# Output projection of a decoder trunk in three rounded products, with w_out loaded early by column halves

## The chip, the cores and the metric

One core of a Trainium2 chip runs the whole kernel. The metric is the time of one execution on the device in microseconds (us), as the median of several runs. The engines are TensorE (PE), VectorE (DVE), ScalarE (ACT), GpSimd (POOL, used only to build constants) and SyncE (SP), whose in-order queue issues all transfers. Every engine works through its own queue in order and waits on semaphores.

## The reference

Two layers over 256 tokens of width 1024, float32. Each layer is a mixer and a mixture of experts, both as residual branches:

```python
def reference(x, ...):
    for layer in range(DEPTH):
        h = rms_norm(x, norm_mix_g[layer])
        if layer % 2 == 0:      # differential + stick-breaking attention
            mix = even_mixer(h, ab_w_in[i], ..., ab_w_out[i], layer)
        else:                   # forgetting attention
            mix = odd_mixer(h, c_w_in[i], c_b_f[i], ..., c_w_out[i])
        x = x + mix
        h = rms_norm(x, norm_ffn_g[layer])
        x = x + hier_moe(h, ...)   # top-1 of 4 groups, top-2 of its 4 experts
    return x

def even_mixer(...):
    proj = h @ w_in                      # 1024 -> 3072
    ...                                  # heads, norms of q and k
    o = jnp.concatenate([from_heads(o_a), from_heads(o_b)], axis=-1)
    return o @ w_out                     # 1024 -> 1024, the output projection
```

## The kernel before

**Stages of a layer.** (1) The tokens are transposed (tokens_across) and multiplied by w_in in six units of 512 columns, two steps j each, so 12 steps. (2) Eight attention jobs j, in turns i: scores, exponentials, transposition of the probabilities or, for the stick-breaking heads B (layer 0, jobs 4 to 7), sums along the map (across), and products with the values (weighted_values). (3) The output projection (out_products) for four pieces q of the output, 128 tokens by 512 columns. (4) Residual adds, norm, router, ranks. (5) The experts: 16 in order, for 64 token slots each, in blocks of four (a quad). The weights of an expert are six units of 2 MB.

**Rounded products.** PE multiplies full float32 in two recorded instructions per product. For the input projection (all units but the first of layer 0) the kernel instead makes of each operand a rounded part (high, type float32r, a copy on ScalarE: weights_high, L656) and the remainder (low, a subtraction on VectorE: weights_low, L1050; tokens_low, L1042), and adds three products: high x high, low x high, high x low (L1556 for the units of v, L1563 for the others). The splits of unit u+1 are queued at an even step j. The output projection of before is in full float32 (L1578): oT holds the attention outputs (over the tile hn), copied out of PSUM by output (L732, ScalarE) or, for B heads, by VectorE (L1286), each with a signal o_ready.

**Slots.** Twelve slots of 2 MB each hold w_in, then expert units. Slots 0 to 5 hold w_in, 6 is free, 7 and 8 lie over qkT and v_sb with attention, 9 and 10 hold the rounded parts w_high and later w_out, 11 lies over hn and hT. Expert unit n of a lap goes to slot n. unit_loaded and unit_used are the semaphores of a slot.

**Order of the queues.** SP issues x, gains, w_in of layer 0, then small parameters (load, L462), then per layer: expert unit u after step 2u+2 into slot u, w_out (L472), slot 6, slot 7 after the last scores, slot 8 after the last attention output, slots 9 and 10 after the output projection, slot 11 after the router. From then on each unit is loaded as soon as its slot is used up. At the end of layer 0 come the units of w_in of layer 1. VectorE at a step j of the projection: root chain or weights_low, root products (L1230), the copy of the step's PSUM bank (L1253, L1244, L1250, signal proj_out), and after the copy of step 4 in layer 0 weights_low of unit 3 and make_tables, which waits for the small parameters. ScalarE at a step: weights_high, then the square of the step's q or k (L777, signal squared); in layer 0 at step 4 it waits for a sum that make_tables forms (L788). PE at step j waits for proj_out of step j-2, and adds up squares in sums (L1495), for the last of them inside step 8 in layer 1 and step 4 in layer 0. mixed_and_normed adds the four pieces to x (L921), ScalarE squares them, and tokens_across brings the sums across for the router.

## Time and profile before

| | us |
|---|---|
| median of 3 runs (1176.65 to 1177.93) | 1177.33 |
| span of the profiled execution | 1175.5 |
| layer 0 before its first expert's first product | 163.2 |
| experts of layer 0, to the last scatter | 587.7 |
| layer 1, first expert's first product | 744.3 |
| last scatter of layer 1 | 1169.2 |

The profiled execution's span runs from its first to its last instruction; the median lies 1.8 us above it, which is what lies around the span and the difference between executions together. Rows of the trace give the start and the duration in us, the engine and the line of the kernel. In a merged row "x8" stands for eight instructions, and the bracket gives the idle time before it and who ended it. PE matmul rows overlap, so the distance between starts is what a product costs in a stream.

### The profile page before, as it was taken

The page shows a single profiled execution, that of the slowest core. Times are in us where ns is not written, and L with a number is a line of the kernel's source. Part 1 is how long each engine was busy: PE and PEld are TensorE (multiplying, and loading weights), DVE is VectorE, ACT ScalarE, POOL GpSimd, SP SyncE. Part 2 cuts the span into 40 slices and gives each one's busy share as a digit, 9 for nine tenths or more (in the row PEclk, how much of TensorE's full clock was granted, in tenths as well). Part 3 has the DMA queues.
Part 4 walks back from the last instruction along what each step waited for, and adds up shares of the span by engine and source line. Part 5 has one row for each costly group of instructions (what it writes and reads, how often), then busy time and mean ns, then how long its engine had stood idle before and what let it go on. Part 6 is the DMA issues. An engine that isn't in the chain of part 4 may idle for free.

```text
span 1175.5 us, 13904 instructions
## 1 busy us (share of the span) xinstructions
PE 1131.3 (96%) x5664; PEld 517.1 (44%) x5664; DVE 431.1 (37%) x776; ACT 175.2 (15%) x347; POOL 7.2 (1%) x36
## 2 busy tenths in 40 slices
PE   8998989999999999999899999899999999999997
PEld 6985433333333333333389754333333333333332
DVE  4656253322222423222285662522223323222222
ACT  4327110000000000000063251000001000000000
POOL 2000000000000000000000000000000000000000
PEclk9999999999999999999999999999999999999999
DMA  9678289999999999999994383999999999999996
GB/s 358 160 324 335 95 324 429 428 427 428 428 430 428 429 428 428 428 428 428 414 397 154 143 345 108 396 428 428 428 428 429 428 429 429 429 428 428 428 429 261
DMA packets 53904, 439.30 MB, mean 374 GB/s; under 512 B 14192, under 2 KB 14192, under 8 KB 29296
## 3 DMA queue, kind: packets, MB, share of 16 engines
q1 hardware_dynamic: 53872, 438.85, 90.0%
q8 instruction: 22, 0.36, 0.1%
q14 instruction: 10, 0.08, 0.0%
HBM read 437.79 MB, written 1.05 MB: 373 GB/s over the span
## 4 chain that ended last, share of the span: by engine, by line
PE 85%; DMA 9%; DVE 3%; ACT 1%; SPq 1%; issue 1%; another core or an unknown queue 0%; ACTq 0%; DVEq 0%
PE bank L1682 50%; PE bank L1563 8%; PE bank L1578 5%; PE bank L1694 5%; PE bank L1661 4%; DMA ring<-in_moe_w_gate 4%; DMA ring<-in_moe_w_up 4%; PE bank L1556 4%; PE bank L1670 1%; PE bank L1725 1%; PE bank L1436 1%; PE bank L1495 1%; PE bank L1718 1%; PE bank L1387 1%; DMA ring<-in_ab_w_in 1%; PE bank L1412 1%
## 5 line engine op out<-in xcount | busy, mean ns | idle before, releaser
L1682 PE MATMUL bank<-ring,work 128*64 128x512 f32 x2304 | 510.9, 594 | 11.3 <-DVE work L1311 6.3
L1682 PEld LDWEIGHTS bank<-ring,work 128*64 128x64 f32 x2304 | 161.6, 137 | 343.6 <-issue 327.3
L1301 DVE TENSOR_SCALAR work<-work 128x512 f32<-128x512 f32 x32 | 13.7, 427 | 456.1 <-ACT work L829 456.1
L1303 DVE RECIPROCAL work<-work 128x512 f32<-128x512 f32 x32 | 107.3, 3353 | 1.1
L832 ACT ACTIVATE attention<-bank 128x512 f32<-128x512 f32 x32 | 19.1, 597 | 531.6 <-PE bank L1682 531.6
L1661 PE MATMUL bank<-x_sb,root_y 128*64 128x512 f32 x272 | 64.2, 593 | 0.0
L1308 DVE TENSOR_TENSOR work<-bank,work 128x512 f32<-128x512 f32 x32 | 22.1, 692 | 113.4 <-PE bank L1682 113.4
L1682 PE MATMUL bank<-ring_over_qk,work 128*64 128x512 f32 x256 | 57.7, 593 | 2.5 <-DMA ring_over_qk<-in_moe_w_gate 2.5
L1682 PE MATMUL bank<-ring_over_v,work 128*64 128x512 f32 x256 | 57.6, 592 | 0.0
L1682 PE MATMUL bank<-ring_spare,work 128*64 128x512 f32 x256 | 57.6, 592 | 0.0
L1578 PE MATMUL bank<-ring,hn 128*128 128x512 f32 x128 | 56.7, 595 | 0.0
L829 ACT ACTIVATE work<-bank 128x512 f32<-128x512 f32 x32 | 19.1, 597 | 227.5 <-PE bank L1682 227.5
L1050 DVE TENSOR_TENSOR w_low<-ring,w_high 128x2048 fp32r<-128x2048 f32 x22 | 49.4, 2285 | 6.7 <-ACT w_high L656 6.6
L656 ACT ACTIVATE w_high<-ring 128x2048 fp32r<-128x2048 f32 x22 | 41.0, 1901 | 11.7 <-PE bank L1563 6.2
L1694 PE MATMUL bank<-attention,root_ln 64*128 64x512 f32 x128 | 31.8, 613 | 6.3 <-ACT attention L832 6.3
L1661 PEld LDWEIGHTS bank<-x_sb,root_y 128*64 128x64 f32 x272 | 19.4, 137 | 39.2 <-issue 37.7
L1578 PEld LDWEIGHTS bank<-ring,hn 128*128 128x128 f32 x128 | 23.7, 190 | 27.5 <-issue 26.9
L1682 PEld LDWEIGHTS bank<-ring_over_qk,work 128*64 128x64 f32 x256 | 18.2, 137 | 39.7 <-issue 35.4
L1682 PEld LDWEIGHTS bank<-ring_spare,work 128*64 128x64 f32 x256 | 18.4, 137 | 36.6 <-issue 36.6
L1682 PEld LDWEIGHTS bank<-ring_over_v,work 128*64 128x64 f32 x256 | 18.4, 137 | 36.6 <-issue 35.7
L1694 PE MATMUL bank<-attention,root_x 64*128 64x512 f32 x128 | 31.8, 615 | 0.0
L1563 PE MATMUL bank<-h_high,w_high 128*128 128x256 f32 x224 | 31.2, 292 | 0.0
(242 smaller groups left out, 930.9 us busy)
## 6 DMA issues: line engine op xcount, KB each, us to landing
ring<-in_moe_w_gate SPq DMA_DIRECT2D x48, 2048.0 KB, 27.1
ring<-in_moe_w_up SPq DMA_DIRECT2D x48, 2048.0 KB, 29.2
ring<-in_moe_w_down SPq DMA_DIRECT2D x48, 2048.0 KB, 27.7
ring_over_qk<-in_moe_w_gate SPq DMA_DIRECT2D x16, 2048.0 KB, 30.4
ring_over_v<-in_moe_w_up SPq DMA_DIRECT2D x16, 2048.0 KB, 30.2
ring_spare<-in_moe_w_down SPq DMA_DIRECT2D x16, 2048.0 KB, 30.9
ring<-in_ab_w_in SPq DMA_DIRECT2D x12, 1024.0 KB, 14.9
ring<-in_c_w_in SPq DMA_DIRECT2D x12, 1024.0 KB, 14.4
```

Source lines behind the costliest of these rows:

```text
L656: act.activation(w_high[u % 2][:, part, :], win_view(u)[:, part, :], ACT.Copy).then_inc(s.w_high, 1)
L829: act.activation(sig, GATE[:, :], ACT.Exp, scale=-1.0).then_inc(s.gate_exp, 1)
L832: act.activation(y, Y[:, :], ACT.Copy).then_inc(s.y_out, 1)
L1050: tt(w_low[u][:, part, :], win_view(u)[:, part, :], w_high[u % 2][:, part, :].bitcast(F32), ALU.subtract).then_inc(s.w_low, 1)
L1303: nc.vector.reciprocal(sig, sig).then_inc(s.gate_step, 1)
L1308: tt(hid, UP[:, :], sig, ALU.mult).then_inc(s.hid_ready, 1)
L1556: last = mm(bank[j % 2][:, :], x_part[:, c, P * t:P * (t + 1)], w[:, c, :], start=(n == 0 and c == 0), stop=(final and c == NC - 1))
L1563: last = mm(bank[j % 2][:, T * half:T * (half + 1)], w[:, c, col:col + P], x_part[:, c, :], start=(n == 0 and half == 0 and c == 0), stop= ...
L1578: last = mm(out_bank(layer, q)[:, :], oT[:, c, P * t:P * (t + 1)], wout_view(c // SUB)[:, c % SUB, HALF * h:HALF * (h + 1)], start=(n == 0 ...
L1661: last = mm(MISC[SLOTS * h:SLOTS * (h + 1), :], take[:, t, :], x_sb[:, t, HALF * h:HALF * (h + 1)], start=(t == 0), stop=(t == NT - 1))
L1682: last = mm(b[SLOTS * half:SLOTS * (half + 1), :], left(h, k), expert_rhs(slot, k, half), start=(h == 0 and k == 0), stop=(h == 1 and k == ...
L1694: mm(ACC[2 * t + half][:, :], giveT[k % 2][r, P * t:P * (t + 1)], y[r, :], start=False, stop=False, skip_group_check=True).then_inc(s.scat ...
```

## The change

The output projection multiplies rounded and remainder parts. For that w_out is loaded by column halves: the first right after the input weights, the second once input unit 0 is done. ScalarE and VectorE split the halves at steps 5 and 7 of the input projection (WOUT_STEPS). The attention outputs are split as they leave PSUM: ScalarE copies them to o_high, VectorE forms o_low; the softmax outputs of layer 0 stay in full in o_rows until their norm is applied and are split after it. ScalarE's output now stands ahead of second in its turn. The pieces q are counted with the token block first (t, h = q % 2, q // 2), their products are interleaved in another order, and three of the four transposes for the router stand between or before the products of the last two pieces. The slots have another numbering in each layer: LAP lists them in the order in which they come free, and expert units are loaded in that order, the first five after steps 8, 10, 10, 12 and 12. Several semaphores are merged (logits_psum, rt_shift, rt_exp, tables_made count for two).

```diff
-OWN, OVER_QK, OVER_V, WOUT = range(UNITS, UNITS + 4)
+OVER_QK, OVER_V = 7, 8
+WIN_SLOTS = ((0, 1, 2, 3, 4, 5), (3, 4, 9, 5, 10, 6))
+HIGH_SLOTS = ((9, 10), (1, 0))
+WOUT_SLOTS = ((6, 0), (2, 3))
+WOUT_HIGH_SLOTS = ((1, 2), (4, 9))
+def lap_of(win, high, wout, wout_high):
+    return (win[3], win[4], high[0], win[5], high[1], OVER_QK, OVER_V, wout[0], wout_high[0],
+            wout[1], wout_high[1], SPARE)
+WOUT_STEPS = (5, 7)
...
 # SP
             for u in range(1, UNITS):
                 load_win(0, u)
+            load_wout(0, 0)
+            sp.wait_ge(layers[0].proj_psum, 2)
+            load_wout(0, 1)
...
-                for u in range(UNITS):
-                    sp.wait_ge(s.proj_psum, STEPS * layer + 2 * u + 2)
-                    load_unit(layer, u, u, 0)
-                load_wout(layer)
-                load_unit(layer, OWN, OWN - UNITS, 1)
+                if layer > 0:
+                    sp.wait_ge(s.proj_psum, STEPS * layer + 2)
+                    load_wout(layer, 1)
+                for i, steps_done in enumerate((8, 10, 10, STEPS, STEPS)):
+                    sp.wait_ge(s.proj_psum, STEPS * layer + steps_done)
+                    load_first(i)
                 sp.wait_ge(s.scores_psum, 2 * JOBS * (layer + 1))
-                load_unit(layer, OVER_QK, OVER_QK - UNITS, 1)
+                load_first(5)
                 sp.wait_ge(s.o_ready, JOBS * layer + JOBS)
-                load_unit(layer, OVER_V, OVER_V - UNITS, 1)
+                load_first(6)
+                sp.wait_ge(s.out_psum, 4 * layer + 2)
+                load_first(7)
+                load_first(8)
                 sp.wait_ge(s.out_psum, 4 * layer + 4)
-                for slot in (WOUT, WOUT + 1):
-                    load_unit(layer, slot, slot - UNITS, 1)
+                load_first(9)
+                load_first(10)
...
 # ScalarE
+            def out_weights_high(layer, h):
+                act.wait_ge(wout_loaded[h], 16 * (layer + 1))
+                act.wait_ge(s.proj_psum, STEPS * layer + 4 + 2 * h)
+                for i in range(2):
+                    act.activation(wout_high(layer, h)[:, part, :], wout_view(layer, h)[:, part, :],
+                                   ACT.Copy).then_inc(s.wout_high, 1)
...
+                act.activation(o_high[:, j, :], O_BANK[:, 0:T], ACT.Copy).then_inc(s.out_high, 1)
...
+                    if j in WOUT_STEPS:
+                        out_weights_high(layer, WOUT_STEPS.index(j))
...
                     if i < JOBS:
                         exponentials(layer, i)
+                    if 2 <= i < JOBS:
+                        output(layer, i - 2)
                     if 1 <= i < JOBS + 1:
                         second(layer, i - 1)
+                    if layer == 0 and i == JOBS:
+                        softmax_outputs_high(s)
+                    if i >= JOBS:
                         output(layer, i - 2)
...
 # VectorE
+            def out_weights_low(layer, h):
+                for i in range(2):
+                    dve.wait_ge(s.wout_high, 4 * layer + 2 * h + i + 1)
+                    tt(wout_low(layer, h)[:, part, :], wout_view(layer, h)[:, part, :],
+                       wout_high(layer, h)[:, part, :].bitcast(F32), ALU.subtract
+                       ).then_inc(s.wout_low, 1)
+            def output_low(layer, j):
+                tt(o_low[:, j, :], O_BANK[:, 0:T], o_high[:, j, :].bitcast(F32), ALU.subtract
+                   ).then_inc(s.o_ready, 1)
...
+                    if j in WOUT_STEPS:
+                        out_weights_low(layer, WOUT_STEPS.index(j))
                     dve.wait_ge(s.proj_psum, STEPS * layer + j + 1)
...
-                        nc.vector.tensor_copy(oT[:, i - 2, :], O_BANK[:, 0:T]).then_inc(s.o_ready, 1)
+                        softmax_outputs_low(s)
+                    if i >= 2 and (layer == 1 or is_b(layer, i - 2)):
+                        output_low(layer, i - 2)
...
 # PE
-                    t, h = q // 2, q % 2
+                    t, h = q % 2, q // 2
+                    if n0 == 0:
+                        pe.wait_ge(s.wout_low, 4 * layer + 2 * h + 2)
                     for n in range(n0, n1):
                         c = chunks[n]
-                        last = mm(out_bank(layer, q)[:, :], oT[:, c, P * t:P * (t + 1)],
-                                  wout_view(c // SUB)[:, c % SUB, HALF * h:HALF * (h + 1)], ...)
+                        for k, (w, o) in enumerate(((high, o_high), (low, o_high), (high, o_low))):
+                            last = mm(out_bank(layer, q)[:, :], o[:, c, P * t:P * (t + 1)], w[:, c, :], ...)
...
                 out_products(0, 0, 2)
                 weighted_values(layer, JOBS - 2)
                 if layer == 0:
                     pe.wait_ge(s.sub_applied, 2)
-                out_products(0, 2, NC - 2)
+                out_products(1, 0, 2)
+                if layer == 1:
+                    out_products(0, 2, 4)
                 weighted_values(layer, JOBS - 1)
-                out_products(0, NC - 2, NC - 1)
+                if layer == 0:
+                    pe.wait_ge(s.sub_applied, 4)
+                    out_products(0, 2, 4)
+                out_products(0, 4, NC - 2)
+                out_products(1, 2, NC - 2)
                 pe.wait_ge(s.o_ready, JOBS * layer + JOBS)
+                out_products(0, NC - 2, NC)
+                out_products(1, NC - 2, NC)
                 pe.wait_ge(s.exp_done, 2 * JOBS * layer + 2 * JOBS)
-                out_products(0, NC - 1, NC)
-                for q in range(1, 4):
-                    out_products(q, 0, NC)
-                    if q == 2:
-                        tokens_across(layer, 1, (0, 1), 0)
+                out_products(2, 0, NC)
+                tokens_across(layer, 1, (0,), 0)
+                out_products(3, 0, 4)
+                tokens_across(layer, 1, (1, 2), 0)
+                out_products(3, 4, NC)
```

## Rows read from the trace of the kernel before

**Rows 1.** Page: the span, and busy us and share of each engine.

```profile
span 1175.5 us, 13904 instructions
...
PE 1131.3 (96%) x5664; PEld 517.1 (44%) x5664; DVE 431.1 (37%) x776; ACT 175.2 (15%) x347; POOL 7.2 (1%) x36
```

**Rows 2.** Chain of waits that ended last: start us, us, what.

```profile
953.84 1.99 PE bank L1694 x8
...
1059.55 1.99 PE bank L1694 x8
...
1090.03 49.41 DMA ring<-in_moe_w_gate
...
1169.15 2.01 PE bank L1694 x8
```

**Rows 3.** Groups by shape: line, operation, count | busy us, mean ns | idle before.

```profile
L1578 PE MATMUL bank<-ring,hn 128*128 128x512 f32 x128 | 56.7, 595 | 0.0
L1050 DVE TENSOR_TENSOR w_low<-ring,w_high 128x2048 fp32r<-128x2048 f32 x22 | 49.4, 2285 | 6.7 <-ACT w_high L656 6.6
L656 ACT ACTIVATE w_high<-ring 128x2048 fp32r<-128x2048 f32 x22 | 41.0, 1901 | 11.7 <-PE bank L1563 6.2 <-DMA ring<-in_ab_w_in 5.1 <-DMA ring<-in_c_w_in 0.3
```

**Rows 4.** Timeline, layer 0, PE: start us, us, line, operation, count [idle before].

```profile
46.23 1.77 PEld L1556 LDWEIGHTS bank<-w_high,h_high 128*128 128x128 f32 x8
...
51.67 2.09 PEld L1563 LDWEIGHTS bank<-h_high,w_high 128*128 128x128 f32 x16
...
119.59 1.88 PE L1578 MATMUL bank<-ring,hn 128*128 128x512 f32 x4
...
150.01 0.63 PE L1342 MATMUL bank<-ident,x_sb 128*128 128x128 f32 x4
```

**Rows 5.** Timeline, layer 0, steps 4 to 7 of the projection.

```profile
52.95 0.17 DVE L956 TENSOR_TENSOR earlier<-desc 128x16 f32<-128x16 f32 x1
...
54.14 0.20 ACT L788 ACTIVATE lam_s<-lam_s 128x2 f32<-128x2 f32 x1 [6.21 <-DVE lam_s L965]
...
56.27 0.75 DVE L1250 TENSOR_SCALAR v_sb<-bank,ssq 128x512 f32<-128x512 f32 x1
...
57.74 0.41 PE L1483 MATMUL bank<-attention,sel_head 96*64 96x256 bf16 x4
```

**Rows 6.** Timeline of SP queue; last, its issues: count, KB, us to landing.

```profile
2.67 24.19 SPq L466 DMA_DIRECT2D ring<-in_ab_w_in  x12
...
39.77 0.43 SPq L462 DMA_DIRECT2D attention<-in_a_lam_k  x1
...
attention<-in_a_lam_k SPq DMA_DIRECT2D x2, 32.0 KB, 3.9
```

**Rows 7.** Timeline, layer 1, steps 5 to 8 of the projection.

```profile
630.22 0.63 ACT L777 ACTIVATE attention<-qkT 128x512 f32<-128x512 f32 x1 [3.36 <-DVE qkT L1253]
...
648.34 0.69 DVE L1253 COPY qkT<-bank 128x512 f32<-128x512 f32 x1 [4.94 <-PE bank L1563]
...
650.84 1.03 PE L1495 MATMUL bank<-attention,slide 128*96 128x256 f32 x4
```

**Rows 8.** Timeline, attention of layer 0, then of layer 1.

```profile
108.02 0.70 PE L1367 MATMUL bank<-qkT 64*128 64x256 f32 x4 [1.45 <-ACT attention L719]
...
690.29 0.56 DVE L1036 COPY attention<-bank 128x384 f32<-128x384 f32 x1 [0.27 <-PE bank L1412]
...
699.98 1.00 PE L1412 MATMUL bank<-ident,attention 128*128 128x128 f32 x6 [1.32 <-DVE attention L1021]
```

**Rows 9.** Stretches: us, busy us of each engine, granted clock, DMA share, GB/s.

```profile
84.00:92.00 8.00, 8.00 (x46) 5.70 (x45) 5.04 (x18) 4.61 (x22) 0.00 (x0) 1.00 0.01 4
165.00:168.00 3.00, 3.00 (x18) 1.04 (x16) 1.11 (x4) 0.00 (x0) 0.00 (x0) 1.00 0.53 224
175.00:560.00 385.00, 378.83 (x1778) 136.11 (x1776) 113.53 (x163) 25.67 (x43) 0.00 (x0) 1.00 1.01 428
```

**Rows 10.** Groups by shape: PE's first products of 512 columns.

```profile
L1349 PE MATMUL bank<-x_sb,ident 128*128 128x512 f32 x2 | 1.9, 1057 | 0.0
```

More of the change, by code:

```diff
@@ L62 @@
 SPARE = RING
-OWN, OVER_QK, OVER_V, WOUT = range(UNITS, UNITS + 4)
+OVER_QK, OVER_V = 7, 8
+PLAIN_SLOTS = (0, 1, 2, 3, 4, 5, 6, 9, 10)
 QUAD = 4
 QUAD_UNITS = QUAD * UNITS
-LAPS = (12, 12)
-SLOT_OF_UNIT = [slot for slots in LAPS for slot in range(slots)]
-PLACES = [(slot, SLOT_OF_UNIT[:i].count(slot)) for i, slot in enumerate(SLOT_OF_UNIT)]
-assert len(PLACES) == QUAD_UNITS and LAPS[0] == RING + 1
-USES = [sum(1 for s, _ in PLACES if s == slot) for slot in range(RING + 1)]
+WIN_SLOTS = ((0, 1, 2, 3, 4, 5), (3, 4, 9, 5, 10, 6))
[5 more added lines that the diff above has]
+            wout[1], wout_high[1], SPARE)
+LAP = tuple(lap_of(*slots) for slots in zip(WIN_SLOTS, HIGH_SLOTS, WOUT_SLOTS, WOUT_HIGH_SLOTS))
+assert all(sorted(lap) == list(range(RING + 1)) for lap in LAP)
+LAPS = QUAD_UNITS // (RING + 1)
+PLACES = [[(lap[i % (RING + 1)], i // (RING + 1)) for i in range(QUAD_UNITS)] for lap in LAP]
+USES = [LAPS] * (RING + 1)
 SLOTS = 64
@@ L173, in trunk @@
         ring, ring_at = [None] * (RING + 1), [None] * (RING + 1)
-        for slot in (*range(UNITS), OWN, WOUT, WOUT + 1):
+        for slot in PLAIN_SLOTS:
             ring[slot] = sb(f"ring{slot}", [P, UNIT])
@@ L315, in trunk @@
         tables_made = sem("tables_made")
-        lam_sums = sem("lam_sums")
         lam_exp = sem("lam_exp")
```

167 lines of the change are left out of this document (98 added, 69 removed).

## The prediction

> **What bounds the kernel now.** I read the page first: TensorE (PE) is busy nearly all of the span [rows 1] and its granted clock is 1.00 in the stretches that I read [rows 9]. That share mixes two kinds of stage, so I read the chain of waits next. In the expert stages the chain runs through PE until near the end of each, then through one weight transfer that was queued for 49 us [rows 2]. The two streams run side by side there. A block of four experts takes PE 1059.55 - 953.84 = 105.71 us when it waits for nothing, so the last scatter of layer 1 would start at 1059.55 + 105.71 = 1165.3; it starts at 1169.15 [rows 2]. The transfers thus cost 3.9 us at the end. Their stream starts when the first expert frees the first slot: just before that the DMA engines stand partly idle (share 0.53), so no backlog is carried in [rows 9]. Both streams are therefore tied to the moment at which the experts start, and whatever moves that moment moves the end of the stage by as much. So I cost everything between the start of a layer and its first expert, where PE works in order and each gap in its stream has a releaser.
>
> **Removed: the full-precision output projection.** Per layer there are 4 outputs of 8 chunks, 32 matmuls of 512 columns, recorded as 64 instructions (128 in two layers) [rows 3]. In layer 0 they run from 119.59 to 150.01 with no gap of note, two value products and two groups of transposes among them: 30.4 us [rows 4]. One transpose group has 4 instructions and takes about 0.6 us, a value product 0.8 us (estimates from the starts around them), so the 64 take 30.4 - 1.1 - 1.6 = 27.7 us, 0.43 each.
>
> **Added on PE: three rounded products.** 96 matmuls of 512 columns per layer. The v projection has the same form (a 128x128 token block held, 512 weight columns streamed, fp32r operands): its 24 matmuls start at 46.23 and the next unit's weights at 51.67, so 5.44 / 24 = 0.227 us each [rows 4]. 96 x 0.227 = 21.8 us. Saved: 27.7 - 21.8 = 5.9, less 0.8 that I allow for a third transpose group that now stands ahead of the last product (its former place hid behind the last residual add): 5.1 us per layer, 10.2 in all. A bound from below: the saving is zero if the held fp32r token parts ran at the price of the removed form; the row of the same form speaks against that.
>
> **Added on ScalarE and VectorE: splitting w_out.** Two column halves per layer, each two copies on ScalarE (1.90 us each) and two subtractions on VectorE (2.29 us each, 4.5 us for the pair back to back) [rows 3], put at steps 5 and 7 of the projection, ahead of the instruction that empties that step's PSUM bank. VectorE's queue is in order, so the bank copy, and behind it PE's step two further on (it waits for proj_out j-1), wait for the subtraction.
> Layer 0, step 5: VectorE has no gap here. It splits unit 3, makes the tables from 52.95, copies step 5 at 56.27, and PE starts step 7 at 57.74 [rows 5]. ScalarE is held for the tables until 54.14 [rows 5], so the first rounded half is there by 54.3 + 1.9 = 56.2, just in time. The subtractions take 56.2 to 60.7, the copy 0.75, and PE starts step 7 at 61.5 to 61.6: +3.85 us. At step 7 of this layer the next 4.5 us find gaps: I follow the queue and each bank copy comes before PE needs it (the copy of step 7 some 1.6 us early).
> Small loads: SP is blocked in issuing the input weights until 26.86 and reaches the last of the four lambda vectors, which the tables wait for, at 39.77; those land in 3.9 us [rows 6]. Two w_out halves of 2 MB now go ahead of them. At the 428 GB/s of the expert stage [rows 9] that is 9.8 us more, so the parameters land near 43.7 + 9.8 = 53.5 instead of 43.7, where the tables began at 52.95: +0.8 us (between 0 and 3, if the blocked issue costs more). The router and forget-gate loads behind them are needed much later. Layer 0 projection: +4.65.
> Layer 1, step 5: ScalarE is free at 630.85, rounds until 634.6; VectorE subtracts until 637.3 and copies the bank after that [rows 7]. PE does not notice. ScalarE's next square and split run some 2.2 us late, and VectorE's copy of step 6 comes at 645.0. Step 7: ScalarE squares step 6 at 645.7 and rounds the second half 646.3 to 650.1; VectorE subtracts 648.25 to 652.75 and copies step 7 at 652.75 instead of 648.34; the square of it ends at 654.1. PE's sums for the head norms, which stood at 650.84 inside step 8 [rows 7], wait for that square and everything behind them on PE too: +3.5 us. The sums start the long root chain on VectorE, so this is not caught up. Both stalls could be smaller (0, if some order lets the copy go first; the code does not) and I keep 0 and 6 as ends for each.
>
> **Attention.** In layer 0 ScalarE is the chain: PE waits 1.45 us for its exponentials at 108.02 [rows 8]. The output copy now stands ahead of them in each turn; with its square it is 0.8 us, and some 0.4 us more comes from the same swap in two turns before. Followed through the queue PE's output products start 1.2 us later. In layer 1 VectorE gets a subtraction of 256 columns in each of eight turns, about 0.4 us (an estimate from its copy of 384 columns, 0.56 us, by two thirds), and in a turn VectorE is idle for 0.27 us [rows 8]. It slips little in the middle and fully in the tail, where PE already waits 1.32 us for VectorE at 699.98 [rows 8]: +1.1 us. Bounds: 0 (the earlier output copy frees ScalarE, a gain that could cover it) and 2.5 each. The rounded parts of the softmax heads (layer 0) come while PE still has other output chunks, 2.7 us of them: nothing; 2 us if that cover goes.
>
> **Transfers.** The first twelve expert units were loaded at steps 2 to 12 and later; now from step 8. DMA is idle after those steps (share 0.01 from 84 to 92) [rows 9], so the later start is free. After the output projection three units follow in both kernels, and the two before them have the 12 us of the last two products for 9.8 us of traffic: no backlog. The input weights of layer 1 wait for slots freed in the same order by the same experts, but for the sixth, whose slot is free long before SP's queue reaches it. Renumbered slots and merged semaphores: nothing.
>
> **Sum.** Layer 0: -5.1 + 4.65 + 1.2 = +0.75. Layer 1: -5.1 + 3.5 + 1.1 = -0.5. Together +0.25 us on the profiled execution's 1175.5 us span [rows 1]. The median of the runs stands 1.8 us above that span, which I keep: 1177.33 + 0.25 = 1177.6. What a measurement can tell from no change is 0.2%, or 2.4 us.
>
> **Rivals.**
> (A) The splits hide. VectorE is busy 37% of the span, ScalarE 15% [rows 1], and the projection steps have gaps; if neither stall reaches PE the sum is -10.2 + 0.8 + 2.3 = -7.1 us, 1170.2; with only one hidden 1173.7 to 1174.1. For it: in layer 1 VectorE is idle for 4.9 us ahead of the copy of step 7 [rows 7]. Against: the queues are in order and the wait of the gap's end is the very bank copy. Chance 0.20.
> (B) Slower: the clock. The two new gaps on PE, 4.65 and 3.5 us, are longer than the waits of 1.3 and 1.5 us that the rows show for PE [rows 8], and PE's first 512-column products after the idle opening took 1057 ns [rows 10] against 595 for the same shape in the output projection [rows 3], nearer to the ratio of 1.2 and 2.4 GHz than to none, although the page grants full speed there too. If PE falls to the lower level in a gap, the next products run at twice their time; one step has 5.4 us of them [rows 4], so a drop costs 1.8 (a third of a step) to 5.4 us more: 1179.4 with one short drop, 1183.0 with one full one, 1188.4 with two. It decides once a gap is long enough for the drop, and no row of before shows a gap that long. Chance 0.12.
> The Trainium skill, TensorE: Matmul & The Clock Gate, "The HAM clock gate", states this rule: the throttled state is the default, and an idle stretch returns PE to half clock until activity releases it. As to the opening the trace agrees with it [rows 10]; for a gap in the middle no row of this case speaks, and if the rule takes hold in both gaps the time would be the 1188.4 of (B), against 1177.6 without it.
> (C) The attention stages turn VectorE- or ScalarE-bound by more than I follow, 2.5 us in each layer instead of 2.3 together, and the softmax cover goes: +4.7, 1182.3. Chance 0.10.
> (D) Transfers arrive late for the first experts: one unit of 2 MB behind costs 4.9 us at each end of stage, 1182.5 for one layer. Against: the count above. Chance 0.05.
> (E) The change does not do what it says: the three products run at 0.43 us each like the removed form, 96 x 0.43 = 41.3 against 21.8, +19.5 per layer, 1216.6. Chance 0.03.
> The forecast holds the remaining 0.50.
>
> **How the numbers follow.** The forecast's own spread is the sizes of two stalls, two attention terms and the parameter load, about 2 us each way: 1175.3 to 1180. The range must leave out at most 2 in 10: I reach down into (A) with one stall hidden and a little under it, 1173.3, and up to the middle of (B), (C) and (D), 1182.5. Faster by over 0.2%: (A), and a little of the forecast, 0.22. Slower by over 0.2%: (B) to (E) nearly whole, 0.28. Within 0.2%: 0.50.
>
> **What the profile after would show.** Right: 192 matmuls of the out_products line about 0.39 us long and 0.227 apart; a wait of PE for VectorE of 4 to 5 us at step 7 in layer 0 and for ScalarE's square of 3 to 4 us at step 8 in layer 1; the first expert about 0.7 us later in layer 0 and 0.3 us later in layer 1 from the start; 3 to 4 us of transfer waits at each end of stage. Wrong: no such waits (A); a granted clock under 1 or 256-column products well over 0.29 us after the gap (B); PE waits for VectorE in each attention turn (C); transfer waits at the first experts (D). The prediction falls if a queue holds an order other than the one I followed, since both stalls rest on the copies being behind the splits.

## The result, and the profile after

The changed kernel takes 1182.74 us (median of 4 runs, 1182.37 to 1183.46) against 1177.28 us for the kernel before: ratio 1.0045, 95% interval 1.0032 to 1.0058. It is slower by 5.5 us, and the forecast was 1177.6 us, range 1173.3 to 1182.5. The profiled execution took 1183.46 us with a span of 1181.7, against 1175.5 before [rows 1].

The page of the changed kernel, its busy times and its slices:

```profile
span 1181.7 us, 14069 instructions
...
PE 1125.6 (95%) x5728; PEld 532.9 (45%) x5728; DVE 452.8 (38%) x794; ACT 192.5 (16%) x361; POOL 7.2 (1%) x36
...
PEclk9989999999999999999999999999999999999999
```

PE is busy for 1125.6 us, 5.7 less than before [rows 1], yet the span is 6.2 longer: the work went down and the idle time up, the more so as the busy time holds slowed products. The clock row has a digit under 9 in slice 3, between 59 and 89 us, which the row of before does not.

Reading where a shift appears is easiest from a table of landmarks, the start in us of the same PE instruction in each profiled execution. The last column is the version without the stalls, of which more below. The sums add up the squares of q or k of each head; the root spread is the product that brings each head's root back over its rows (the one with sel_head).

| landmark on PE | before | after | difference | without the stalls |
|---|---|---|---|---|
| L0 projection, step 2, first rounded product | 26.68 | 27.15 | +0.5 | 26.88 |
| L0 step 7 | 57.74 | 64.41 | +6.7 | 57.94 |
| L0 step 8 | 64.03 | 72.51 | +8.5 | 64.23 |
| L0 first product of the output projection | 119.59 | 129.54 | +10.0 | 121.31 |
| L0 first gather of an expert | 158.92 | 163.71 | +4.8 | 155.48 |
| L1 first transpose | 589.65 | 594.15 | +4.5 | 586.21 |
| L1 last sums (in step 8) | 650.84 | 658.30 | +7.5 | 647.42 |
| L1 first root spread (in step 9) | 659.09 | 668.21 | +9.1 | 655.67 |
| L1 first product of the output projection | 700.82 | 710.76 | +9.9 | 698.02 |
| L1 first gather of an expert | 740.09 | 746.27 | +6.2 | 732.17 |
| end of the span | 1175.5 | 1181.7 | +6.2 | 1167.3 |

Between the landmarks: layer 0 loses 6.2 us up to step 7, 1.8 in step 7 itself, 1.5 in attention and wins 5.2 in the output projection; layer 1 loses 3.0 up to the sums, 1.7 in step 8, 0.8 in attention and wins only 3.8 in the output projection. The expert stages keep their length within 0.3 us.

**The output projection.** By shape, two of the three products of the changed kernel (the third, with h_low, has 64 more) and the split of w_out (line, operation, tiles, count, busy us, mean ns, idle before):

```profile
L1673 PE MATMUL bank<-rounded,h_high 128*128 128x512 f32 x128 | 41.5, 406 | 0.0
...
L1124 DVE TENSOR_TENSOR rounded<-ring,rounded 128x2048 fp32r<-128x2048 f32 x8 | 18.0, 2288 | 5.0 <-ACT rounded L707 5.0
```

The mean of 406 ns is that of the overlapped products; 60 of them in a row took 13.83 us, 0.23 each. The split has the durations of the input weights' split in [rows 3].

**Layer 0, the wait at step 7.** The timeline of SP's queue in the changed kernel (start us, us, engine, line, operation, count [idle before <- releaser]):

```profile
26.90 9.28 SPq L499 DMA_DIRECT2D ring<-in_ab_w_out  x2
36.22 5.94 SPq L490 DMA_DIRECT2D g_qk<-in_a_q_gain  x2
...
51.69 0.43 SPq L490 DMA_DIRECT2D attention<-in_a_lam_k  x1
```

The same first pair of small loads in the kernel before:

```profile
26.91 4.04 SPq L462 DMA_DIRECT2D g_qk<-in_a_q_gain  x2
```

And the changed kernel's timeline of all engines behind that:

```profile
55.87 0.18 DVE L1022 TENSOR_TENSOR earlier<-desc 128x16 f32<-128x16 f32 x1 [2.36 <-DMA attention<-in_a_lam_k]
...
57.17 3.69 ACT L707 ACTIVATE rounded<-ring 128x2048 fp32r<-128x2048 f32 x2
...
59.19 4.50 DVE L1124 TENSOR_TENSOR rounded<-ring,rounded 128x2048 fp32r<-128x2048 f32 x2
...
63.61 0.74 DVE L1341 TENSOR_SCALAR v_sb<-bank,ssq 128x512 f32<-128x512 f32 x1
...
64.41 0.64 PE L1574 MATMUL bank<-attention,sel_head 96*64 96x256 bf16 x4 [6.12 <-DVE v_sb L1341]
...
72.51 0.41 PE L1574 MATMUL bank<-attention,sel_head 96*64 96x256 bf16 x4
```

SP stood 9.28 us in issuing the two halves of w_out and 5.94 us in the first small loads behind them, 1.9 more than before; the last lambda vector was issued at 51.69, not at 39.77 [rows 6], and the tables began at 55.87, not at 52.95 [rows 5]. ScalarE, which waits for the tables, rounded from 57.17, VectorE subtracted 59.19 to 63.69, the bank copy came at 63.61, and PE had waited 6.12 us. Then step 7 took 72.51 - 64.41 = 8.10 us; before it took 6.29. The stretches show why (us, busy us of PE, of its weight loads PEld, of DVE, ACT and POOL, each with its number of instructions, granted clock, DMA share, GB/s):

```profile
62.00:64.00 2.00, 0.00 (x0) 0.00 (x0) 2.00 (x2) 2.00 (x2) 0.00 (x0) 0.50 0.37 34
...
66.00:68.00 2.00, 2.00 (x11) 2.00 (x11) 2.00 (x2) 2.00 (x2) 0.00 (x0) 0.50 0.17 16
...
70.00:72.00 2.00, 2.00 (x19) 2.00 (x18) 2.00 (x2) 0.00 (x0) 0.00 (x0) 1.00 0.03 8
...
660.00:662.00 2.00, 2.00 (x6) 1.52 (x6) 1.07 (x3) 1.97 (x3) 0.00 (x0) 0.50 0.00 0
...
712.00:714.00 2.00, 2.00 (x8) 1.08 (x9) 0.00 (x0) 0.00 (x0) 0.00 (x0) 0.56 0.00 0
714.00:716.00 2.00, 2.00 (x15) 1.49 (x12) 0.42 (x1) 0.39 (x1) 0.00 (x0) 1.00 0.00 0
```

The granted clock fell to 0.50, the lower of the two levels, while PE stood idle, and was back at 1.00 by 70.00. It fell twice more in layer 1: from 659 on, behind the wait for the last sums, and from about 710 on, in the output projection, behind the waits at the end of attention. In these two PE was at work again when the clock fell: from 656 to 658, where PE stood idle, it was still 1.00. All four timed runs have a mean granted clock of 0.994 or 0.995, so the drops are not those of the profiled execution alone.

**Layer 1, the wait before the sums.** The timeline of all engines in the changed kernel:

```profile
652.40 4.49 DVE L1124 TENSOR_TENSOR rounded<-ring,rounded 128x2048 fp32r<-128x2048 f32 x2 [2.50 <-ACT rounded L707]
...
656.81 0.69 DVE L1344 COPY qkT<-bank 128x512 f32<-128x512 f32 x1
657.52 0.63 ACT L839 ACTIVATE attention<-qkT 128x512 f32<-128x512 f32 x1 [3.36 <-DVE qkT L1344]
...
658.30 1.17 PE L1586 MATMUL bank<-attention,slide 128*96 128x256 f32 x4 [2.78 <-ACT attention L839]
```

Rounding, subtraction, bank copy, square, sums: each starts when the one ahead of it is done, in the order that the prediction followed in [rows 7].

### The profile page after: what moved, and what is told of

It reads as the page before. It is cut to its first block, busy times and chain, and to the rows that moved or that the text cites. A ratio compares the mean times of both kernels' runs of the same rounds, so it can differ in the third digit from the quotient of the medians.

```text
span 1181.7 us, 14069 instructions
## 1 busy us (share of the span) xinstructions
PE 1125.6 (95%) x5728; PEld 532.9 (45%) x5728; DVE 452.8 (38%) x794; ACT 192.5 (16%) x361; POOL 7.2 (1%) x36
## 4 chain that ended last, share of the span: by engine, by line
PE 78%; DMA 9%; DVE 7%; ACT 2%; SPq 2%; issue 1%; another core or an unknown queue 0%; ACTq 0%; DVEq 0%
PE bank L1782 50%; PE bank L1654 5%; PE bank L1794 5%; PE bank L1761 4%; DMA ring_over_v<-in_moe_w_gate 4%; DMA ring<-in_moe_w_up 4%; PE bank L1673 4%; PE bank L1647 3%; SPq L490 1%; PE bank L1770 1%; PE bank L1825 1%; DVE rounded L1124 1%; DVE rounded L1116 1%; PE bank L1818 1%; PE bank L1527 1%
## 5 line engine op out<-in xcount | busy, mean ns | idle before, releaser
L1654 PE MATMUL bank<-h_high,rounded 128*128 128x256 f32 x448 | 59.9, 293 | 0.0
L1654 PEld LDWEIGHTS bank<-h_high,rounded 128*128 128x128 f32 x448 | 57.0, 196 | 1.8 <-issue 0.8
L1116 DVE TENSOR_TENSOR rounded<-ring,rounded 128x2048 fp32r<-128x2048 f32 x22 | 49.4, 2285 | 5.3 <-ACT rounded L698 5.3
L698 ACT ACTIVATE rounded<-ring 128x2048 fp32r<-128x2048 f32 x22 | 41.0, 1901 | 10.7 <-DMA ring<-in_ab_w_in 5.7
L1673 PE MATMUL bank<-rounded,h_high 128*128 128x512 f32 x128 | 41.5, 406 | 0.0
L1647 PE MATMUL bank<-rounded,h_high 128*128 128x512 f32 x128 | 33.5, 413 | 0.0
## 6 DMA issues: line engine op xcount, KB each, us to landing
ring<-in_moe_w_down SPq DMA_DIRECT2D x32, 2048.0 KB, 27.7
```

Source lines behind the costliest of these rows:

```text
L698: act.activation(w_high(layer, u)[:, part, :], win_view(layer, u)[:, part, :], ACT.Copy).then_inc(s.w_high, 1)
L1116: tt(w_low(layer, u)[:, part, :], win_view(layer, u)[:, part, :], w_high(layer, u)[:, part, :].bitcast(F32), ALU.subtract).then_inc(s.w_lo ...
L1647: last = mm(bank[j % 2][:, :], x_part[:, c, P * t:P * (t + 1)], w[:, c, :], start=(n == 0 and c == 0), stop=(final and c == NC - 1))
L1654: last = mm(bank[j % 2][:, T * half:T * (half + 1)], w[:, c, col:col + P], x_part[:, c, :], start=(n == 0 and half == 0 and c == 0), stop= ...
L1673: last = mm(out_bank(layer, q)[:, :], o[:, c, P * t:P * (t + 1)], w[:, c, :], start=(n == 0 and k == 0), stop=(n == NC - 1 and k == 2))
```

## Experiments

All are edits to the changed kernel but for the last two, which edit the kernel before. Ratios are to the kernel before on the same chip, with the 95% interval; the changed kernel itself stands at 1.0045.

### The parameters first

```diff
-            load_wout(0, 0)
-            sp.wait_ge(layers[0].proj_psum, 2)
-            load_wout(0, 1)
             for i, (q, k) in enumerate(((a_q_gain, a_k_gain), (c_q_gain, c_k_gain))):
...
                 load(lam_in[:, j, :], g[0].partition_broadcast(P), params_loaded)
+            load_wout(0, 0)
+            sp.wait_ge(layers[0].proj_psum, 2)
+            load_wout(0, 1)
```

> The changed kernel with one edit: in SP's queue of layer 0 the small parameters (gains, the four lambda vectors) stand ahead of the two halves of w_out. Theory (the wait of 6.12 us at step 7 is my predicted stall behind the subtraction, lengthened because the tables started at 55.87 instead of 52.95): the tables start near 53 again, the wait falls to 3.2 to 4.0 us and the time by 2.4 to 2.9 us, from 1182.7 to about 1180.1; if the shorter wait also spares the clock, by 4.2 us. Rival (the parameters are beside the path, and the subtraction or w_out itself ends the wait): the wait stays near 6 us and the time moves by less than 0.5 us; if w_out then lands late, it grows.

Measured 1180.87 us, ratio 1.0021 (1.0007 to 1.0035): 0.24 percentage points below the changed kernel, 2.8 us. PE's timeline:

```profile
61.74 0.41 PE L1574 MATMUL bank<-attention,sel_head 96*64 96x256 bf16 x4 [3.67 <-DVE v_sb L1341]
...
69.50 0.41 PE L1574 MATMUL bank<-attention,sel_head 96*64 96x256 bf16 x4
```

The wait fell to 3.67 us, as the theory says, and the clock fell all the same (0.50 from 64 to 66): step 7 took 7.76 us. It also fell in layer 0's attention here, behind a wait of 2.17 us, and before the sums of layer 1. The 3.85 us that I had predicted for the subtraction alone were nearly right; the parameters account for the rest.

### Layer 0: splits at steps 7 and 9, behind the bank copies

```diff
-WOUT_STEPS = (5, 7)
+WOUT_STEPS = ((7, 9), (5, 7))
+LATER = (True, False)
...
-                    if j in WOUT_STEPS:
-                        out_weights_low(layer, WOUT_STEPS.index(j))
+                    if j in WOUT_STEPS[layer] and not LATER[layer]:
+                        out_weights_low(layer, WOUT_STEPS[layer].index(j))
                     dve.wait_ge(s.proj_psum, STEPS * layer + j + 1)
...
+                    if layer == 0 and j in WOUT_STEPS[layer]:    # behind the copy of step j
+                        out_weights_low(layer, WOUT_STEPS[layer].index(j))
```

> The changed kernel, layer 0 only: ScalarE rounds w_out at steps 7 and 9, and VectorE subtracts behind the bank copy of steps 7 and 9, not ahead of those of 5 and 7; the order of the loads stays. Theory (the in-order queue makes the wait): the wait of PE at step 7 falls from 6.12 us to what the late parameters alone leave, 1.6 to 2.4 us, the products behind it run at full clock, and the time falls by 3.8 + 1.7 = 5.5 us to about 1177.2. Rival 1 (the late parameters hold the whole wait): it stays over 5 us and the time moves under 1 us. Rival 2 (the splits only move their stall to a later step or to the attention): the step 7 wait goes, the first expert starts no earlier.

Measured 1177.86 us, ratio 1.0001 (0.9990 to 1.0012), 5.2 us less than the changed kernel. PE's timeline, then stretches:

```profile
59.77 0.41 PE L1577 MATMUL bank<-attention,sel_head 96*64 96x256 bf16 x4 [1.94 <-DVE v_sb L1342]
...
67.53 0.41 PE L1577 MATMUL bank<-attention,sel_head 96*64 96x256 bf16 x4
```

```profile
60.00:64.00 4.00, 4.00 (x24) 3.89 (x21) 4.00 (x2) 4.00 (x3) 0.00 (x0) 0.57 0.38 36
...
108.00:110.00 2.00, 2.00 (x7) 1.33 (x7) 0.69 (x2) 1.79 (x4) 0.00 (x0) 0.50 0.06 16
```

The wait that is left, 1.94 us, is that of the late parameters alone (the prediction had +0.8 for them, and 3 as its end). My expectation was wrong in one point: even this wait was followed by a lower clock, and step 7 took 7.76 us. The clock then fell a second time, in attention. Layer 0's first gather came 4.8 us earlier than in the changed kernel, of which 4.2 us are the wait and 0.5 the opening; this execution has two drops in the layer, the changed kernel's has one.

### Layer 1: splits where VectorE is idle

```diff
-WOUT_STEPS = (5, 7)
+WOUT_STEPS = ((5, 7), (5, 8))    # ScalarE's
+LATER = (False, True)    # True: no subtraction ahead of the copies, as above
...
+                    if layer == 1 and j in (5, 9):    # behind the copy of step j
+                        out_weights_low(layer, *((0,) if j == 5 else (1, (0,))))
...
                         second(layer, 0)
+                        if layer == 1:
+                            out_weights_low(layer, 1, (1,))
```

> The changed kernel, layer 1 only: VectorE subtracts the first half of w_out behind the bank copy of step 5; ScalarE rounds the second half at step 8, behind the last input weights, and VectorE subtracts it in two pieces, behind the copy of step 9 and at step 11. Theory (the wait of 2.78 us before the last sums is the split ahead of the copy of step 7, and the clock falls after it): the wait goes or is under 0.5 us, the granted clock stays at 1.00 in step 8, and the time falls by 2.8 to 4.6 us to 1178.1 to 1179.9. Rival (the pieces delay the roots or the attention instead, both on VectorE): the wait goes and the attention of layer 1 starts no earlier, time within 1 us of 1182.7.

Measured 1180.36 us, ratio 1.0023 (1.0014 to 1.0032), 2.6 us less, a little under the 2.8 to 4.6 that I expected. The sums stood at 655.84 with no wait ahead of them and the clock at 1.00; the root spread came 8.25 us after the sums, as in the kernel before. The rival had a part, too: PE now waited for VectorE at the first scores. PE's timeline:

```profile
655.84 1.03 PE L1591 MATMUL bank<-attention,slide 128*96 128x256 f32 x4
...
664.09 1.06 PE L1579 MATMUL bank<-attention,sel_head 96*64 96x256 bf16 x16
...
675.22 0.32 PE L1476 MATMUL bank<-cum_neg,sel_head 96*128 96x384 bf16 x1 [1.34 <-DVE qkT L1320]
```

### Waits kept, PE kept busy

```diff
+                    if layer == 0 and j == 7:
+                        unread_products(O_BANK, x_sb[:, 0, 0:COLS], 6)
                     if j >= 2:
                         pe.wait_ge(s.proj_out, STEPS * layer + j - 1)
...
                         if j == normed and n == 1:
+                            if layer == 1:
+                                unread_products(O_BANK, x_sb[:, 0, 0:COLS], 3)
                             sums(j)
```

> The changed kernel with products that nobody reads put into PE's two gaps: six of 128x128 by 512 columns of fp32 ahead of the wait of step 7 in layer 0, three ahead of the last sums in layer 1. The waits themselves and all work that counts stay. Theory of the clock (the products behind each gap ran at 1.2 GHz because PE had stood idle: step 7 took 7.54 us where others take 5.95): the granted clock stays at 1.00, step 7 takes 5.95 us again, and the time falls by 1.6 us for each gap, 3.3 us in all, to 1179.4. Rival (the slow products waited for something else, or the clock falls anyway): no gain, 1182.7, or some tenths more where the unread products outlast the wait.

Measured 1180.22 us, ratio 1.0023 (1.0014 to 1.0033), 2.6 us less. PE's timeline in layer 0; the first row is the unread products:

```profile
58.15 5.32 PE L1440 MATMUL bank<-x_sb,ident 128*128 128x512 f32 x12
65.00 0.41 PE L1574 MATMUL bank<-attention,sel_head 96*64 96x256 bf16 x4 [1.53 <-DVE v_sb L1341]
...
71.28 0.41 PE L1574 MATMUL bank<-attention,sel_head 96*64 96x256 bf16 x4
```

The same in layer 1, then stretches:

```profile
658.64 1.10 PE L1586 MATMUL bank<-attention,slide 128*96 128x256 f32 x4
...
666.98 1.06 PE L1574 MATMUL bank<-attention,sel_head 96*64 96x256 bf16 x16
```

```profile
64.00:68.00 4.00, 3.00 (x26) 2.81 (x27) 4.00 (x4) 4.00 (x3) 0.00 (x0) 1.00 0.36 36
...
660.00:664.00 4.00, 4.00 (x19) 3.26 (x19) 2.85 (x9) 3.73 (x4) 0.00 (x0) 1.00 0.03 8
...
116.00:118.00 2.00, 2.00 (x12) 1.43 (x14) 0.36 (x1) 1.94 (x4) 0.00 (x0) 0.50 0.00 0
```

This is the run that isolates the clock. The work that counts waits as long as before, and yet step 7 takes 6.28 us and the stretch from the sums to the root spread 8.34, against 8.10 and 9.91 in the changed kernel. The median is 2.6 us lower where I expected 3.3, which the intervals cannot tell apart. The two profiled executions lie 3.1 us apart (1178.6 against 1181.7). Each has a drop in attention as well, here in layer 0 behind a wait of 2.17 us (last row), there in layer 1, and here step 7 began 0.6 us later, since the tables did (56.46 against 55.87). The timed runs say the same without a profile: three of the twelve have a mean granted clock of 1.000 and took 1178.3 to 1179.2 us, the nine at 0.997 or 0.998 took 1179.1 to 1182.3. With the waits kept and no drop at all, the change thus costs 1.3 to 2.1 us over the 1177.06 of the kernel before.

### Both stalls taken away

```diff
-WOUT_STEPS = (5, 7)
+WOUT_HIGH_STEPS = ((7, 9), (5, 6))
+WOUT_LOW_STEPS = (((7, 0), (7, 1), (9, 2), (9, 3)), ((5, 0), (5, 1), (6, 2), (7, 3)))
...
-                    if j in WOUT_STEPS:
-                        out_weights_low(layer, WOUT_STEPS.index(j))
...
                         nc.vector.tensor_copy(dst, bank[j % 2][:, :]).then_inc(s.proj_out, 1)
+                    for step, part in WOUT_LOW_STEPS[layer]:
+                        if step == j:
+                            out_weights_low(layer, part // 2, (part % 2,))
```

with the parameters first.

> The changed kernel with both stalls taken away: in layer 0 the parameters are loaded ahead of w_out, ScalarE rounds w_out at steps 7 and 9 and VectorE subtracts behind those steps' bank copies; in layer 1 ScalarE rounds the second half at step 6 ahead of its square, where the trace of the version with layer 1's splits later shows it idle for 5.16 us, and VectorE's four pieces stand behind the copies of steps 5 (two), 6 and 7, in idle stretches of 4.9, 3.1 and 2.9 us. Theory (stalls, late parameters and the clock are all of the loss; the saving of 5.3 us a layer is real): PE waits under 0.5 us at both places, the clock stays at 1.00, the time is 1182.5 - 6.1 - 1.6 in layer 0 and - 2.8 - 1.6 in layer 1, so 1170.4, 1169.5 to 1171.5, faster than the kernel before by 0.5 to 0.65%. Rival (what the stalls took comes back later, at the transfers at the ends of the expert stages): the first experts start 12 us earlier in all, the last scatter by less than 8, time 1174 or more.

Measured 1170.02 us, ratio 0.9931 (0.9915 to 0.9947): faster than both kernels, 7.0 us less than before by the medians. Rival (A), in which neither split reaches PE, had 1170.2, with 0.8 in it for late parameters that this version does not have. PE's waits in layer 0's projection are gone and the clock stays at 1.00 (60 to 68):

```profile
29.57 4.18 PE L1656 MATMUL bank<-h_high,rounded 128*128 128x256 f32 x32
...
60.64 0.41 PE L1576 MATMUL bank<-attention,sel_head 96*64 96x256 bf16 x4
...
66.92 0.41 PE L1576 MATMUL bank<-attention,sel_head 96*64 96x256 bf16 x4
```

The profiled execution began late, however (step 2 at 29.57), so the same kernel ran again.

> The version without the two stalls once more, unchanged. Its profiled execution began 2.9 us later than the kernel before's (third step at 29.57, not 26.68) and showed the clock at 1.00 in both attention stages, although the same waits stand there behind which other executions showed 0.56 to 0.79. Theory (opening and attention clock differ from execution to execution): median 1169 to 1171, ratio 0.993; third step between 26.6 and 30.7; the clock may fall in one attention stage, for 1.3 to 1.6 us. Rival (the later opening belongs to this kernel's loads): the third step starts at 29 or later again.

Measured 1170.21 us, ratio 0.9950 (0.9934 to 0.9967), step 2 at 26.88: the late opening belongs to that execution. Its landmarks are the last column of the table. The end of its span is 8.2 us earlier than before; the rival of the transfers falls, since the stage from the first gather of layer 0 to layer 1's first transpose took 430.7 us in this version as in the kernel before.

### ScalarE's order in attention

```diff
-                    if 2 <= i < JOBS:
-                        output(layer, i - 2)
                     if 1 <= i < JOBS + 1:
                         second(layer, i - 1)
...
-                    if i >= JOBS:
+                    if i >= 2:
                         output(layer, i - 2)
```

> The changed kernel with only that edit to ScalarE's order. By my attention term PE's wait of 2.17 us for ScalarE at the scores of layer 0 falls to about 1.4, its wait of 1.14 us at the third output products goes, and the time falls by 1.0 to 1.4 us to 1181.2. Rival: no change, 1182.5, or slower by up to 1 us where VectorE then gets its outputs later.

Measured 1183.54 us, ratio 1.0043 (1.0026 to 1.0060): no change, where my term asked for 1.0 to 1.4 us less. Waits of PE in layer 0's attention (line waited for, us in total, times, longest), the changed kernel first, then this one:

```profile
PE bank L1458 <- ACT attention L770: 2.2, 1, 2.2
PE bank L1527 <- ACT hT L784: 1.1, 1, 1.1
...
PE bank L1527 <- ACT attention L770: 0.6, 1, 0.6
```

```profile
PE bank L1456 <- ACT attention L770: 1.5, 1, 1.5
PE bank L1525 <- DVE h_low L1129: 1.4, 1, 1.4
```

The wait of 2.2 us went down to 1.5, the level of [rows 8]; but one of 1.4 us for VectorE's subtraction took the place of one of 0.6. So the output projection began 28.1 us after the third scores (PE's first work behind the bank copy of the last step), against 27.7 in the changed kernel and 26.2 before. My term for layer 0 (1.2 predicted, 1.5 measured) had the right size and half the cause. With the stalls taken away the same edit told as little:

> The same, and ScalarE's queue in attention in the order of the kernel before: each output copy behind the second exponentials or copy of its turn, not ahead of it. Theory of my attention term (in layer 0 the output copy with its square stands ahead of what PE waits for): 1.0 to 1.4 us faster than without this edit, from layer 0; in layer 1 no change or up to 0.5 us slower, since the subtraction then starts later. Rival (the 1.4 us in layer 0's attention come from the w_out splits or from the subtraction on VectorE): no change or slower.

Measured 1169.38 us, ratio 0.9928 (0.9912 to 0.9944), the same as without the edit. If the order only trades one wait for the other, each kind of head should have its own:

```diff
+                    behind = i >= JOBS or layer == 0 and i - 2 < A_HEADS
+                    if i >= 2 and not behind:
+                        output(layer, i - 2)
                     if 1 <= i < JOBS + 1:
                         second(layer, i - 1)
...
+                    if i >= 2 and behind:
                         output(layer, i - 2)
```

> The version without the two stalls, and ScalarE's order in layer 0's attention mixed: the outputs of the four softmax heads, each with its square, behind the second step of the turn as in the kernel before; those of the other heads ahead of it as in the changed kernel. Theory (the 1.47 us that layer 0's attention lost are two parts that the order trades against each other: output copy and square ahead of what PE's scores wait for, or the rounded copy and VectorE's subtraction late for the value products): PE's wait of 2.17 us for ScalarE falls to 1.46, that of 0.58 us at the value products does not grow to the 1.41 it had with the order of before, and the output products start 0.6 to 1.0 us earlier after the third scores than 27.68 us. On the time 0.8 us, less than a comparison can tell. Rival (the queues realign and another engine ends the same waits): 27.5 us or more.

Measured 1169.41 us, ratio 0.9938 (0.9925 to 0.9951). The wait for ScalarE is at 1.45 us and the one at the value products still at 0.58; from the third scores to the output projection it took 27.03 us instead of 27.68:

```profile
108.37 0.70 PE L1461 MATMUL bank<-qkT 64*128 64x256 f32 x4 [1.45 <-ACT attention L771]
...
113.39 0.87 PE L1530 MATMUL bank<-attention,v_sb 128*64 128x256 f32 x8 [0.58 <-ACT attention L771]
```

The time cannot tell 0.65 us; the traces can, with one execution each. Of the 1.5 us that layer 0's attention lost (27.68 against 26.2), the order explains these 0.65; where the other 0.8 come from no run shows.

### The subtractions of the outputs

```diff
-                tt(o_low[:, j, :], O_BANK[:, 0:T], o_high[:, j, :].bitcast(F32), ALU.subtract
+                tt(o_low[:, j, 0:8], O_BANK[:, 0:8], o_high[:, j, 0:8].bitcast(F32), ALU.subtract
```

> The changed kernel with VectorE's subtraction of each rounded output cut from 256 to 8 columns, so that the remainders of the others are left out of the output. It takes some 0.35 us from each of eight turns of layer 1 and of four of layer 0. My term says 1.1 us of the subtractions reach PE in layer 1, in the tail, where it waits 1.65 us for VectorE: 0.7 to 1.2 us faster, and with the shorter waits the granted clock (0.72 and 0.78 behind them) back at 1.00, another 0.8 to 1.5 us: 1179.8 to 1181.8. Rival (VectorE has room for them): no change, 1182.5.

Measured 1181.49 us, ratio 1.0036 (1.0024 to 1.0048). That lies in the range of my term, but the interval holds the changed kernel's 1.0045 too, so the time is no evidence. In the trace PE's two waits for VectorE at the end of layer 1's attention are 1.39 and 0.8 us, against 1.65 and 1.1: the subtractions cost that place 0.55 us, half of my 1.1. The clock stayed at 1.00 there, but so it did in the version without the stalls, where both waits are as long as in the changed kernel; what the subtraction has to do with the clock is not settled by this.

### The wait alone, in the kernel before

```diff
+                    if layer == 0 and j == 5:
+                        unread_sum = ring[OWN][:, :].rearrange("p (c n) -> p c n", c=NC)
+                        for i in range(2):    # range(1) in the second kernel
+                            part = slice(SUB * i, SUB * (i + 1))
+                            tt(unread_sum[:, part, :], w_high[1][:, part, :].bitcast(F32),
+                               w_high[1][:, part, :].bitcast(F32), ALU.subtract)
                     dve.wait_ge(s.proj_psum, STEPS * layer + j + 1)
```

> The kernel before, and nothing of the change but its wait: VectorE makes two subtractions of 128x2048 (4.5 us, read by nobody) ahead of the bank copy of step 5 in layer 0, where the changed kernel subtracts the first half of w_out. Theory (the stall costs its wait and a clock drop behind it): PE waits 3.7 us at step 7 as in the version with the parameters first, the granted clock goes to 0.50 and step 7 takes 7.8 us instead of 6.29; time 1177.1 + 3.7 + 1.5 = 1182.3, ratio 1.0044. Rival (only the wait counts, and the rest of that loss belonged to the change's loads or slots): step 7 takes 6.29 us, 1180.8, ratio 1.0031.

Measured 1183.45 us, ratio 1.0047 (1.0033 to 1.0061).

> The same with one subtraction (2.25 us), so that the wait is about 1.4 us, shorter than any at this place so far (1.94 us already cost 1.5 us of clock there). If the price of the clock is one drop or none, whatever the wait: either step 7 takes 6.29 us and the time is 1177.1 + 1.4 = 1178.5, ratio 1.0012, or 7.8 us and 1180.0, ratio 1.0025. I expect the first, because waits of 1.3 to 1.5 us stand in the kernel before at full clock. Rival (the price grows with the wait): step 7 takes 6.6 to 6.9 us, in between.

Measured 1178.80 us, ratio 1.0012 (1.0003 to 1.0021). With two subtractions, PE's timeline and a stretch:

```profile
61.36 0.64 PE L1489 MATMUL bank<-attention,sel_head 96*64 96x256 bf16 x4 [3.67 <-DVE v_sb L1256]
...
70.38 0.41 PE L1489 MATMUL bank<-attention,sel_head 96*64 96x256 bf16 x4
```

```profile
64.00:66.00 2.00, 2.00 (x12) 2.00 (x11) 2.00 (x2) 0.00 (x0) 0.00 (x0) 0.50 0.99 426
```

And with one subtraction:

```profile
59.38 0.41 PE L1489 MATMUL bank<-attention,sel_head 96*64 96x256 bf16 x4 [1.46 <-DVE v_sb L1256]
...
65.67 0.41 PE L1489 MATMUL bank<-attention,sel_head 96*64 96x256 bf16 x4
```

A wait of 3.67 us made step 7 take 9.02 us; one of 1.46 us left it at 6.29, with the clock at 1.00. Two useless instructions on an engine that is busy for 37% of the span cost as much as the whole change did.

## Why the prediction was wrong

**Saving on PE (5.1 us a layer): right.** From the output projection's start to the first gather it is 39.33 us before and 34.17 after in layer 0, and 39.27 and 34.15 in layer 1 of the version without the stalls: 5.2 and 5.1. (E) falls.

**Stall at step 7, layer 0 (4.65): right in place and cause, too small.** The part of the subtraction was 3.85 predicted and 3.67 measured, with the parameters first and again in the kernel before. The part of the parameters was predicted at 0.8; it was 1.94 alone and 6.12 - 3.67 = 2.45 on top of the subtraction. The step that failed is the landing time of 53.5, worked out from bytes over bandwidth: the tables, which wait for the parameters, began at 55.87. What counts is when SP can issue. Its queue stood 9.28 us in issuing w_out and 5.94 instead of 4.04 us in the first small loads, and issued the last lambda vector 11.9 us later than before, not 9.8.

**Stall in layer 1 (3.5): right.** 2.78 us of wait, 3.0 on the landmarks. (A) falls with both.

**Attention (1.2 and 1.1):** 1.5 and 0.8 measured, with layer 0's cause only half seen, as told above. (C) falls: together 2.3, as forecast, and for layer 0 that is in part luck. **Transfers (0):** right, and (D) falls.

**The clock (0 in the sum, rival B with a chance of 0.12): this is where the prediction failed.** In the profiled execution it cost 8.10 - 6.29 = 1.81 us in step 7 of layer 0, 9.91 - 8.25 = 1.66 between sums and root spread in layer 1, and 35.51 - 34.15 = 1.36 in layer 1's output projection, in all 4.8. With the measured sizes and no clock, layer 0 comes to 6.2 + 1.5 - 5.2 = +2.5, layer 1 to 3.0 + 0.8 - 5.1 = -1.3, the opening to +0.5 and the first expert stage to -0.3: +1.4 on the span of 1175.5, where the forecast had +0.25. The clock's 4.8 bring it to the 1181.7 that was measured. Without them the time would be 1177.3 + 1.4 = 1178.7, inside the stated range; the filled version's runs at a full clock, 1178.3 to 1179.2, say the same. The reasoning of (B) named the rule, the place and the price of a short drop (1.8). It failed in its weight: I had two waits of 3.5 us or more in my own sum, no row of the kernel before with a wait that long, and still put the case that they cost nothing but themselves at four times the chance of the case that they don't. The Trainium skill, TensorE: Matmul & The Clock Gate, "The HAM clock gate", says that an idle stretch returns PE to half clock, and the traces agree, 1.00 to 0.50 behind each new wait of 1.94 us or more in the projection stages. My 1188.4 for two drops was too high since each cost 1.7 us and not 5.4.

## What to carry to other kernels

Work that is put into a gap of an in-order queue must be ready when the gap opens: the 4.9 us ahead of step 7's bank copy in [rows 7] were enough for 4.5 us of subtraction, but ScalarE's half came 2.5 us late (the idle time in the row of 652.40), and the copy behind it waited; with the second half rounded a step earlier and the subtractions put directly behind the copies, the same work cost PE no wait in the projection. A new wait on TensorE costs its length and, in every execution here in which it was 1.94 us or more in the projection, a slower clock behind it; where the sum contains a wait longer than any that the old trace shows at full clock, the drop belongs in the forecast and not among the rivals. And small loads that gate a table go ahead of large ones that nobody needs yet, since they pay for the time in which the queue stands in issuing, not only for the bytes.

## What I had not expected of the hardware

- The price of a clock drop did not grow with the wait: step 7 took 7.76, 7.76 and 8.10 us after waits of 1.94, 3.67 and 6.12 us, and 9.02 after another of 3.67; 6.29 after 1.46 or none. It went with how much of step 7 fell into the low stretch: the mean granted clock over step 7 was 0.78, 0.78, 0.74 and 0.65. In the changed kernel a part of the low stretch passed while PE still waited and cost nothing. These are one execution each. The rows of step 7 in the changed kernel and behind two useless subtractions:

```profile
64.41:72.51 8.10, 8.10 (x52) 7.58 (x53) 8.10 (x6) 3.65 (x3) 0.00 (x0) 0.74 0.12 13
```

```profile
61.36:70.38 9.02, 9.02 (x53) 8.50 (x54) 5.60 (x4) 0.00 (x0) 0.00 (x0) 0.65 0.98 421
```

- In attention the same waits are followed by a drop in some executions and not in others: behind the 2.17 us of layer 0 the clock fell in the filled version (0.50) and with the parameters first, and not in the changed kernel; behind the 1.65 us of layer 1 it fell in the changed kernel (0.56) and not in the version without the stalls. In the two versions that put one layer's splits later it fell in layer 0's attention behind a wait of 1.13 us, shorter than the 1.46 that cost nothing at step 7. So no single length of wait parts the cases. What decides stays open.
- The opening differs between executions of one kernel by 2.7 us (step 2 at 29.57 and 26.88), so a span is compared from a landmark behind it. In the late execution the first input weights landed 1.3 us later (PE's first product on them at 12.72, not 11.42), and then the clock fell here too: step 0 took 8.40 us, not 7.01. The stretch in the late execution:

```profile
12.00:16.00 4.00, 3.27 (x9) 2.69 (x10) 0.89 (x5) 0.00 (x0) 0.00 (x0) 0.57 1.05 397
```
